# Six score levels of a gated recurrence in strips of 32 columns instead of 64, and the sampled states' products in four strips instead of two

## The reference, cut to what matters

```python
def _hgrn2_chunk_scan(q, k, v, log_f, s0):   # per chunk:
        b = jnp.cumsum(gc, axis=1)
        o_inter = jnp.einsum('bthk,bhkv->bthv', qc * jnp.exp(b), S)
        decay = jnp.where(causal, jnp.exp(b[:, :, None] - b[:, None, :]), 0.0)
        scores = jnp.einsum('bthk,btshk,bshk->bths', qc, decay, kc)
        o_intra = jnp.einsum('bths,bshv->bthv', scores, vc)
        S_new = jnp.exp(b_end)[..., None] * S + jnp.einsum(
            'bshk,bshv->bhkv', kc * jnp.exp(b_end[:, None] - b), vc)
```

## Time and profile before

| | us |
|---|---|
| median of three runs | 2186.64 |
| the profiled execution, whole | 2188.33 |
| its span, first to last instruction | 2186.6 |
| TensorE busy in the span | 2142.7 |
| VectorE busy | 1600.6 |
| ScalarE busy | 906.9 |

### The profile page before, as it was taken

The page is one execution under the profiler, slowest core; times in us unless marked ns, Lnnn a source line. Parts: engine busy times, 40 slices in busy tenths (PEclk is TensorE's granted clock), DMA queues, the critical chain, the costliest instruction groups (busy, mean ns, idle before and its releaser), DMA issues.

```text
span 2186.6 us, 42987 instructions
## 1 busy us (share of the span) xinstructions
PE 2142.7 (98%) x17360; PEld 2108.6 (96%) x17360; DVE 1600.6 (73%) x2462; ACT 906.9 (41%) x1284; POOL 5.7 (0%) x19
## 2 busy tenths in 40 slices
PE   9999999999999989999999999999989999999998
PEld 8999999999999889999999999999988999999998
DVE  5766776457878789778487887848797579686774
ACT  5222232234545455445155543515533345253443
POOL 0000000000000000000000000000000000000000
PEclk9999999999999999999999999999999999999999
DMA  5233543243242144445245242424374434242332
GB/s 142 77 90 105 161 128 108 73 116 80 60 117 60 52 117 113 129 125 146 63 128 138 68 124 85 142 64 116 109 218 149 108 91 124 84 137 87 97 88 81
DMA packets 439814, 234.91 MB, mean 107 GB/s; under 512 B 34849, under 2 KB 432370, under 8 KB 439666
## 3 DMA queue, kind: packets, MB, share of 16 engines
q1 hardware_dynamic: 426562, 218.76, 35.5%
q10 hardware_dynamic: 12528, 13.08, 1.8%
q0 software_dynamic: 576, 1.05, 0.3%
HBM read 212.67 MB, written 23.30 MB: 108 GB/s over the span
## 4 chain that ended last, share of the span: by engine, by line
PE 93%; DVE 5%; issue 1%; DMA 1%; ACT 1%; SPq 0%; DVEq 0%; ACTq 0%
PE ps L2519 52%; PE ps L2631 33%; PE ps L2748 2%; PE ps L2482 1%; PE ps L2938 1%; PE ps L2927 1%; PE ps L2913 0%; PE ps L2826 0%; DVE w_lo L1500 0%; DVE o_rs L2243 0%; DMA w_raw<-in_ffn_w_in_dram 0%; DMA wb<-wb_d 0%; PE ps L2790 0%; PE ps L2799 0%; PE ps L2817 0%
## 5 line engine op out<-in xcount | busy, mean ns | idle before, releaser
L2631 PE MATMUL ps<-hf_hi,s_hi 128*128 128x288 f32 x1848 | 547.6, 296 | 9.6 <-issue 4.5
L2631 PE MATMUL ps<-hf_lo,s_hi 128*128 128x288 f32 x1848 | 543.2, 294 | 0.0
L2631 PE MATMUL ps<-hf_hi,s_lo 128*128 128x288 f32 x1848 | 542.5, 294 | 0.0
L2631 PEld LDWEIGHTS ps<-hf_hi,s_hi 128*128 128x128 f32 x1848 | 346.9, 188 | 12.6 <-issue 7.2
L2631 PEld LDWEIGHTS ps<-hf_lo,s_hi 128*128 128x128 f32 x1848 | 347.2, 188 | 0.2
L2631 PEld LDWEIGHTS ps<-hf_hi,s_lo 128*128 128x128 f32 x1848 | 346.9, 188 | 0.0
L1588 DVE TENSOR_TENSOR s_lo<-s_raw,s_hi 128x1024 fp32r<-128x1024 f32 (+1 forms) x264 | 286.5, 1089 | 60.6 <-ACT s_hi L987 52.9
L987 ACT ACTIVATE s_hi<-s_raw 128x1024 fp32r<-128x1024 f32 (+1 forms) x264 | 250.2, 950 | 191.5 <-PE ps L2631 183.2
L929 ACT ACTIVATE w_hi<-w_raw 128x1024 fp32r<-128x1024 f32 (+4 forms) x141 | 185.7, 1323 | 242.4 <-PE ps L2519 239.4
L2519 PE MATMUL ps<-h_hi,w_hi 128*128 128x288 f32 x1216 | 267.8, 302 | 2.2 <-issue 1.1
L2519 PE MATMUL ps<-h_hi,w_lo 128*128 128x288 f32 x1216 | 260.5, 296 | 0.0
(11 more groups left out here) (415 smaller groups left out, 3081.1 us busy)
## 6 DMA issues: line engine op xcount, KB each, us to landing
s_raw<-in_ffn_w_in_dram SPq DMA_DIRECT2D x330, 256.0 KB, 3.3
w_raw<-in_ffn_w_out_dram SPq DMA_DIRECT2D x96, 256.0 KB, 3.2
w_raw<-in_ffn_w_in_dram SPq DMA_DIRECT2D x44, 512.0 KB, 5.1
w_raw<-in_hgrn_w_in_dram SPq DMA_DIRECT2D x32, 512.0 KB, 5.4
w_raw<-in_ffn_w_out_dram SPq DMA_DIRECT2D x48, 192.0 KB, 2.6
w_raw<-in_s_w_glu_dram SPq DMA_DIRECT2D x16, 512.0 KB, 5.1
w_raw<-in_ffn_w_out_dram SPq DMA_DIRECT2D x16, 384.0 KB, 4.0
w_raw<-in_ffn_w_out_dram SPq DMA_DIRECT2D x16, 320.0 KB, 3.7
```

The costliest lines, as they stand in the source:

```text
L2631: ins = M.matmul(out, w, h, start=f in (0, 1, 3) and k == 0 and n == 0, stop=f in (3, 5, 6) and k == KP - 1 and n == 2, skip_group_check=True)
```

## The change

Levels 0 to 5 are taken as four products of 32 keys by 32 queries for each chunk, in four column strips. Levels 6 and 7 and the sampled tokens' scores stay as they are. In the tail each sequence's incoming state is taken as four products of 32 value columns for two of 64.

```diff
-                    last, side = n == LEVELS - 1, P // 2
+                    last, side = n == LEVELS - 1, P // 2 if n >= LEVELS - 2 else P // 4
                     for c in range(CHUNKS):
-                        for key in range(1 if last else 2):
+                        for key in range(1 if last else P // side):
                             keys = slice(c * P + side * key, c * P + side * (key + 1))
                             at = slice(c * P + side, (c + 1) * P) if last else keys
                             ins = M.matmul(ps[side * key:side * (key + 1), 4 + n % 2, at], k[:, keys],
                                            q[:, at], start=True, stop=True)
...
-                        for c in range(2):
-                            side = slice(P // 2 * c, P // 2 * (c + 1))
+                        for c in range(4):
+                            side = slice(P // 4 * c, P // 4 * (c + 1))
                             ins = M.matmul(ps[side, 4, n * DEC_SEQ:(n + 1) * DEC_SEQ], s_in[b][:, n, side],
                                            q_t[b][:, at:at + DEC_SEQ], start=False, stop=n == DEC_BATCH - 1)
```

## The result

The changed kernel takes 2192.09 us (median of 17 runs, 2189.23 to 2196.42); the kernel before, run beside it, 2187.69 (17 runs, 2186.15 to 2190.15). The ratio is 1.0019, 95% interval 1.0012 to 1.0026: 4.4 us slower. The forecast was 3.4 us faster, with a range that ended at 2188.0. The profiled execution of the changed kernel is one of its faster runs: 2189.70 us, span 2188.0, 1.4 us more than the span before.

The account below looks back on a forecast made before the run. TensorE, holding 93% of the chain of waits, was taken to bound the kernel. Levels 0 to 3 (0.6), levels 4 and 5 (0.8) and the tail (2.0) summed to 3.4 us less, 2183.2 us; range 2176.5 to 2188.

Parts of the forecast that it names:

- At no cost: Whole kernel: masked copies, DMA, waits and queues unchanged; 64 more products a head covered by instructions issued ahead; no cost.
- The tail: Sampled tokens' incoming states: 0.42 us a head, less at the loop's branch, nothing in heads 6 and 7; 2.0 us saved.
- Levels 0 to 3: 16 places: narrow products gain 0.42 us each, changes of shape around the sampled product take most back; 0.6 us saved.
- The rival without a drain: Levels 0 to 3: no drain between narrow shapes, each place keeps 0.42 us; 9.5 us saved in all, 2177.1; chance 0.17.
- Levels 4 and 5: 0.42 us a head, lost in heads 1 to 5 waiting for ScalarE's root, kept in heads 0 and 6; 0.8 us saved.
- The issue rival: TensorE's issue: records no faster than 29 ns in a long run, so doubling them costs 30 us, 2217; chance 0.10.

Follow-up runs that it names:

- sampled_strips: The changed kernel with TensorE's loop written out and the sampled scores of levels 0 to 3 as two 32 by 32 blocks: 2175.63 us, 0.9939 of the kernel before.
- plain_long: The kernel before, without narrow tiles, its loop kept and levels 0 and 1 computed twice: 2201.25 us, ratio 1.0054.

## Why the prediction was wrong, point by point

- *The step that failed* is "At no cost": "The doubled products (64 more a head) are covered by what the sequencer issues ahead." Their issue was covered: records come 7 ns apart. But each product is also four instructions in a loop's body, which grew from 1625 to 2137 with a limit just above 1625. The tail's step named the branch and took its 211 ns as fixed; it took 3794 ns, and the slow clock behind it another 1.47 us. The same step's "No DMA, wait or queue moves" fell with it: the instruction queue moved ten blocks between the branches, where it had moved none. I read no row of the instruction queue. Its silence between the loop's two branches would have said that the loop ran from a buffer, and so that its length was a resource.
- *Levels 0 to 3*: 0.6 forecast; the first product behind such a place moves by 0.00 to 0.03 us. The mechanism was right, the price of the changes of shape a little low: 126, 107 and 151 ns in a place, and sampled_strips shows 0.51 us when they go and the sampled product is narrow too. The rival without a drain falls.
- *Levels 4 and 5*: 0.39 to 0.41 us gained a head (0.42 forecast), 0.30 to 0.32 given back behind ScalarE's root in heads 1 to 5: 0.09 to 0.10 kept, at the end of my 0 to 0.1. Heads 0 and 6 keep theirs.
- *The tail*: 0.34 us in heads 1 and 3, 0.38 in head 5 (0.42 forecast), 0.23 and 0.21 in heads 0 and 4 (0.36 and 0.30). Behind the tail of head 6 TensorE waits for VectorE as before, now 2.2 us (1.8 in the earlier trace rows), and in the closing step 2.8 (2.4), so most of what the tails of heads 6 and 7 gain ends in these waits:

```profile
PE ps L2826 <- DVE s_out L2223: 2.8, 1, 2.8
PE ps L2748 <- DVE ssq L2235: 2.2, 1, 2.2
```

- *The sum*: 3.4 us forecast. From the start of the stage (+0.01 us against before) to 831 us (+0.53) the starts lose 0.52; without the 5.1 of the branch and the slow stretch they would have gained 4.6. Nothing in the sum was off by as much as the term that was missing.
- *The issue rival* (2217 us) named TensorE's front end, but in another form: 29 ns a record did not come, 64 records start within 0.7 us. The Trainium skill, "TensorE: Matmul & The Clock Gate", Back-to-back issue gap, gives about 25 ns as the least distance of such products; here they start 7 ns apart within a group of four strips, so the measurement decides against it for strips.
- *The range* took in no case with an idle TensorE, and so ended at 2188.0. The chance of 0.10 for slower rested on that one rival.

The profiled execution shows 5.1 us for the branch and what follows, and a span only 1.4 longer, 0.9 of it from another mixer, where TensorE waits 1.8 us at 1661 us of the span instead of 0.7; over all runs the medians lie 4.4 apart. The 17 runs spread over 7.2 us, and the mean clock falls with the time (0.993 to 0.995 in the five fastest, 0.990 to 0.991 in the three slowest). That the slow stretch behind the stall differs from run to run would fit this; with one profile of the changed kernel it is not shown.

## What to carry to other kernels

Before instructions are added to a loop, look at the instruction queue in its second round: if it is silent, the body runs from the buffer, and its length is a limit like any other; write the loop out, or keep the body short. When small tiles are made smaller, change everything that stands between them to the same shape, or look whether each change of shape takes the gain back, as here. And price what follows an idle engine as well as the idle time.

## What the runs showed of the hardware

- A loop of 1625 instructions on TensorE ran its second round with no block fetched; with 64 more (1689) it fetched nine, and its back-branch took 3.6 us instead of 0.21. Beyond that the price does not grow much: 3.35 to 3.8 us up to 2137 instructions.
- After 3.4 to 4 us idle, TensorE ran at the 1.2 GHz level: for 3.4 us in the changed kernel, for 9.3 from its restart in plain_long, whose products were being fed late as well (4.99 of 6.28 us busy).
- Code fetched in sequence did not show: the written-out kernels fetch 7 to 9 blocks from 598 to 676 us, where the loop fetched one, and TensorE is busy all through 590 to 606 us. Outside the span it may cost a little: 1.7 to 3.0 us lie around the span in the runs of the written-out kernels (sampled_strips apart, with 1.7 to 1.8), 1.7 to 1.8 in those with the loop.
- 32 records of 32 columns in four strips start within 0.26 us, 64 of them with 8 tokens within 0.7; at a change of shape in between, the next start comes 0.13 to 0.15 us later.
